# Expert weights in 8 KB pieces, four y buffers, and the residual x in the projections' operand region

## The reference

```python
mod = silu(c) @ ada_w + ada_b                    # shift1, scale1, gate1, shift2, scale2, gate2
u = x * (1 + scale1) + shift1
q, k, v, lru_x, lru_gate, gate_a, gate_b = split(u @ w_in)           # w_in 1024 x 5376
y = sigmoid(gate_a) * sliding_window_attention(q, k, v) \
  + sigmoid(gate_b) * rg_lru(lru_x) * gelu(lru_gate)
x = layer_norm(alpha * x + gate1 * (y @ w_out))
u = x * (1 + scale2) + shift2
# router: softmax(u @ router_w + router_b), one of 4 groups, the 2 best of its 4 experts, weights w
f = sum over the two experts e of w_e * (silu(u @ w_gate[e]) * (u @ w_up[e])) @ w_down[e]
x = layer_norm(alpha * x + gate2 * f)
```

## Time and profile before

| | |
|---|---|
| runs | median 803.24 us (801.51 to 806.11, 3 runs) |
| profiled execution | 802.2 us; from its first to its last instruction 800.0 us |
| mean granted TensorE clock | 0.921 of full |
| busy share | TensorE 82%, VectorE 43%, ScalarE 31%, GpSimd 12% |
| DMA | 189.37 MB, mean 237 GB/s |
| weights' DMAs | 32 each for gate, up and down, 1 MB each; 13.7, 17.3 and 15.1 us from issue to landing (medians) |
| stores of y | 40, 128 KB each |

### The profile page before, as it was taken

The page is one execution under the profiler, slowest core; times in us unless marked ns, Lnnn a source line. Parts: engine busy times, 40 slices in busy tenths (PEclk is TensorE's granted clock), DMA queues, the critical chain, the costliest instruction groups (busy, mean ns, idle before and its releaser), DMA issues.

```text
span 800.0 us, 15178 instructions
## 1 busy us (share of the span) xinstructions
PE 654.3 (82%) x5985; PEld 423.9 (53%) x5986; DVE 341.1 (43%) x657; ACT 251.0 (31%) x522; POOL 97.2 (12%) x184
## 2 busy tenths in 40 slices
PE   0799999999987999999895297979997769999800
PEld 0376666777755777777683144434553334555400
DVE  0355554587888776757545632000110000111148
ACT  0334433747454655545013011111111111111144
POOL 0221000200000000000000231211221111222230
PEclk9999999999989999999996589898998798999955
DMA  9999766461312232237918999999998999982162
GB/s 303 377 282 317 246 237 210 154 215 55 103 54 67 72 90 63 79 106 257 373 53 300 395 346 401 398 353 365 344 341 320 382 329 389 343 307 75 43 215 105
DMA packets 110033, 189.37 MB, mean 237 GB/s; under 512 B 4968, under 2 KB 57416, under 8 KB 106928
## 3 DMA queue, kind: packets, MB, share of 16 engines
q1 hardware_dynamic: 96288, 149.05, 53.4%
q0 software_dynamic: 7264, 31.87, 11.2%
q10 hardware_dynamic: 6448, 8.00, 2.8%
HBM read 175.23 MB, written 13.67 MB: 236 GB/s over the span
## 4 chain that ended last, share of the span: by engine, by line
PE 48%; DMA 18%; DVE 13%; SPq 11%; ACT 5%; issue 4%; POOL 0%; ACTq 0%; POOLq 0%; DVEq 0%
PE psum L1482 11%; DMA wu<-in_moe_w_up_dram 9%; SPq L387 7%; PE psum L1290 6%; DMA raw<-in_w_in_dram 6%; PE psum L1291 6%; PE psum L1292 6%; PE psum L1493 6%; SPq L392 2%; PE psum L1256 2%; SPq L401 1%; PE psum L1333 1%; DMA x<-in_x_dram 1%; PE psum L1465 1%; ACT ssb L729 1%
## 5 line engine op out<-in xcount | busy, mean ns | idle before, releaser
L1482 PE MATMUL psum<-wg,xs 128*32 128x256 f32 x1280 | 158.9, 402 | 27.2 <-DMA wu<-in_moe_w_up_dram 25.3
L1482 PE MATMUL psum<-wu,xs 128*32 128x256 f32 x1280 | 158.3, 402 | 0.0
L1290 PE MATMUL psum<-uh,whi 128*128 128x512 f32 x336 | 137.8, 410 | 1.6 <-DVE wlo L875 1.5
L1291 PE MATMUL psum<-ul,whi 128*128 128x512 f32 x336 | 131.2, 391 | 0.0
L1292 PE MATMUL psum<-uh,wlo 128*128 128x512 f32 x336 | 131.1, 390 | 0.0
L1482 PEld LDWEIGHTS psum<-wg,xs 128*32 128x32 f32 x1280 | 75.1, 114 | 86.3 <-DMA wu<-in_moe_w_up_dram 28.9
L1189 DVE TENSOR_TENSOR h_sb<-psum,hsil 64x256 f32<-64x256 f32 x40 | 17.1, 427 | 187.0 <-ACT hsil L786 187.0
L875 DVE TENSOR_TENSOR wlo<-raw,whi 128x1024 fp32r<-128x1024 f32 x42 | 51.4, 1224 | 69.1 <-ACT whi L613 68.9
L1493 PE MATMUL psum<-wd,hT 128*32 128x256 f32 x1280 | 78.6, 387 | 0.4 <-DVE hT L1193 0.4
L1290 PEld LDWEIGHTS psum<-uh,whi 128*128 128x128 f32 x336 | 63.4, 189 | 22.8 <-issue 7.4
L786 ACT ACTIVATE hsil<-psum 64x256 f32<-64x256 f32 x40 | 15.1, 376 | 187.0 <-PE psum L1482 187.0
(11 more groups left out here) (258 smaller groups left out, 833.1 us busy)
## 6 DMA issues: line engine op xcount, KB each, us to landing
wg<-in_moe_w_gate_dram SPq DMA_DIRECT2D x32, 1024.0 KB, 13.7
wu<-in_moe_w_up_dram SPq DMA_DIRECT2D x32, 1024.0 KB, 17.3
wd<-in_moe_w_down_dram SPq DMA_DIRECT2D x32, 1024.0 KB, 15.1
raw<-in_w_in_dram SPq DMA_DIRECT2D x42, 512.0 KB, 3.9
ada<-in_ada_w_dram POOLq DMA_DIRECT2D x16, 1024.0 KB, 6.8
ada<-in_ada_w_dram SPq DMA_DIRECT2D x8, 1024.0 KB, 17.4
y_d<-ysb ACTq DMA_DIRECT2D x40, 128.0 KB
y_d<-zrow POOLq DMA_DIRECT2D x8, 512.0 KB, 6.4
```

What stands on the lines that cost most here:

```text
L1290: mmul(bank[s % 2], h[:, k, :], uh[:, k, :], start=(k == 0), stop=False)
L1291: mmul(bank[s % 2], h[:, k, :], ul[:, k, :], start=False, stop=False)
L1482: ins = mmul(psum[32 * g:32 * g + 32, 0, 0:256], xs[:, k % 2, k // 2, :], wgu[slot][g // 2][:, k, (g % 2) * 256:(g % 2) * 256 + 256], star ...
```

## The change

1. The contraction orders are turned: partition p holds rows 8p to 8p + 7 of w_gate and w_up (of w_down, two neighbouring rows of each half), so that the part of a 1 MB DMA that goes to one partition is one piece of 8 KB. For this u2 is written in a turned column order, the router's weights are read in the same order, and h is transposed with a step of two.
2. Four y buffers with four semaphores in place of two, and ScalarE's loop goes over four blocks at a time, after four written out ahead of it. The spare rows of y_d are three blocks more, with one more store of zeros.
3. x1 moves from R_Q to R_U (uh's place), and its loads go out as soon as the projections are done, ahead of the weights; slot 0's gate weights move to R_Q, and their first load comes behind the wait for y_lo. Other homes of slot weights and of the last stage's tiles follow.

```diff
@@ homes
-        x1, _ = at(R_Q, "x1", [P, NT, D])
+        x1, _ = at(R_U, "x1", [P, NT, D])
-        for i, o_ in enumerate((R_U, R_Z, R_B)):
+        for i, homes in enumerate(((R_Q, R_U + 16 * KB, R_Y), (R_Z, R_Z + 16 * KB, R_T), (R_B, R_W, R_W + 16 * KB))):
...
-        for i in range(2):
-            t_, o = at(o, f"ysb{i}", [P, 256])
-            ysb.append(t_)
+        ysb = [at(R_W + 32 * KB + KB * i, f"ysb{i}", [P, 256])[0] for i in range(4)]
@@ weights
-        wg_v = moe_w_gate[0].rearrange("e (k p) f -> e p k f", p=P)
-        wu_v = moe_w_up[0].rearrange("e (k p) f -> e p k f", p=P)
-        wd_v = moe_w_down[0].rearrange("e (k p) n -> e p k n", p=P)
+        wg_v = moe_w_gate[0].rearrange("e (p k) f -> e p k f", p=P)
+        wu_v = moe_w_up[0].rearrange("e (p k) f -> e p k f", p=P)
+        wd_v = moe_w_down[0].rearrange("e (a p c) n -> e p a c n", p=P, c=2)
@@ SyncE, behind the projections
             sp.wait_ge(S["proj_ps"], NPROJ)
-            sp.dma_start(a2r[:, :], row_of(3)).then_inc(rows_in, 16)
-            sp.dma_start(b2r[:, :], row_of(1)).then_inc(rows_in, 16)
-            load_gate_up(sp, 0, 0, 0)
-            sp.wait_ge(S["y_lo"], KT)
             for t in range(NT):
                 sp.dma_start(x1[:, t, :], x[0, t * P:(t + 1) * P, :]).then_inc(x1_in, 16)
-
+                if t == 0:
+                    sp.dma_start(a2r[:, :], row_of(3)).then_inc(rows_in, 16)
+                    sp.dma_start(b2r[:, :], row_of(1)).then_inc(rows_in, 16)
+            sp.wait_ge(S["y_lo"], KT)
+            load_gate_up(sp, 0, 0, 0)
             load_gate_up(sp, 0, 0, 1)
@@ ScalarE's loop
-            with act.Fori(2, nblk, 2) as b:
-                gated(b)
-                x_columns(b + 1)
-                y_out(b - 1, 1, b * 8)
-                gated(b + 1)
-                x_columns(b + 2)
-                y_out(b, 0, b * 8 + 16)
+            with act.Fori(4, nblk, 4) as b:
+                for j in range(4):
+                    gated(b + j)
+                    x_columns(b + (j + 1))
+                    if j == 0:
+                        y_out(b - 1, 3, b * 4)
+                    else:
+                        y_out(b + (j - 1), j - 1, b * 4 + 16)
@@ VectorE's u2, TensorE's h_transpose
-                V.scalar_tensor_tensor(u2[t % 2][:, :], zt[:, :], rstd[:, t:t + 1], b2r[:, :], ALU.mult, ALU.add)\
-                    .then_inc(S["u2_done"], 1)
+                V.scalar_tensor_tensor(u2[t % 2][:, :].rearrange("t (k p) -> t p k", k=KT), by_k(zt), rstd[:, t:t + 1],
+                                       by_k(b2r), ALU.mult, ALU.add).then_inc(S["u2_done"], 1)
...
-                    ins = nc.tensor.transpose(bank[2][:, c * 64:(c + 1) * 64], h_sb[64:128, c * P:(c + 1) * P],
+                    ins = nc.tensor.transpose(bank[2][:, c * 64:(c + 1) * 64], h_sb[64:128, bass.ds(c, P, 2)],
                                               ident[64:128, 64:128])
```

More of the change, by code:

```diff
@@ L116, in hybrid_layer @@
     u2_d = dram("u2_d", [T, D])
-    y_d = dram("y_d", [(NBLK + 1) * SUB, D])
+    y_d = dram("y_d", [(NBLK + 4) * SUB, D])
     ctx = ExitStack()
@@ L305, in hybrid_layer @@
         wgu, wdn = [], []
-        for i, o_ in enumerate((R_U, R_Z, R_B)):
-            wgu.append([at(o_ + 16 * KB * m, f"w{'gu'[m]}{i}", [P, KT, FF])[0] for m in range(2)])
-            wdn.append(at(o_ + 32 * KB, f"wd{i}", [P, FT, D])[0])
-        assert R_Z + 48 * KB <= R_T + 16 * KB
+        for i, homes in enumerate(((R_Q, R_U + 16 * KB, R_Y), (R_Z, R_Z + 16 * KB, R_T), (R_B, R_W, R_W + 16 * KB))):
+            wgu.append([at(homes[m], f"w{'gu'[m]}{i}", [P, KT, FF])[0] for m in range(2)])
+            wdn.append(at(homes[2], f"wd{i}", [P, FT, D])[0])
+        assert R_Z + 32 * KB == R_T and R_B + 16 * KB == R_W
         o = R_T + 16 * KB
@@ L319, in hybrid_layer @@
         hT, o = at(o, "hT", [P, 2, 2, SUB])
-        ysb = []
-        for i in range(2):
-            t_, o = at(o, f"ysb{i}", [P, 256])
-            ysb.append(t_)
+        ysb = [at(R_W + 32 * KB + KB * i, f"ysb{i}", [P, 256])[0] for i in range(4)]
         gate2r, o = at(o, "gate2r", [P, D])
@@ L331, in hybrid_layer @@
         fsum = small("fsum", [P, NT, 3])
-        fin = [[at(R_U + 12 * KB * i + 4 * KB * j, f"fin{i}{j}", [P, D])[0] for j in range(3)] for i in range(NT)]
+        fin = [[at(home + 4 * KB * i, f"fin{i}{j}", [P, D])[0] for j, home in enumerate((R_Q, R_U + 16 * KB, R_Y))]
+               for i in range(NT)]
         psum = ctx.enter_context(nc.psum_tensor("psum", [P, 8, 512], F32))
@@ L360, in hybrid_layer @@
         u2_st = [sem(f"u2_st{i}") for i in range(2)]
-        y_st = [sem(f"y_st{i}") for i in range(2)]
+        y_st = [sem(f"y_st{i}") for i in range(4)]
         out_st = sem("out_st")
@@ L390, in load_down @@
             for half in range(2):
-                ks = slice(2 * half, 2 * half + 2)
-                sp.dma_start(wdn[slot][:, ks, :], wd_v[e][:, ks, :]).then_inc(dn_in[slot], 16)
+                sp.dma_start(wdn[slot][:, 2 * half:2 * half + 2, :], wd_v[e][:, half, :, :]).then_inc(dn_in[slot], 16)
         @block.sync
@@ L527, in _ @@
                                            v[0, g * 512:(g + 1) * 512].partition_broadcast(32)).then_inc(late_in, 16)
-                    pool.dma_start(rw[:, :, 0:NE], router_w.rearrange("(k p) e -> p k e", p=P)).then_inc(late_in, 16)
+                    pool.dma_start(rw[:, :, 0:NE], router_w.rearrange("(p k) e -> p k e", p=P)).then_inc(late_in, 16)
                     pool.dma_start(rbr[:, :], router_b.rearrange("(a e) -> a e", a=1)).then_inc(late_in, 16)
@@ L539, in _ @@
                 pool.dma_start(y_d[(NE + 4 * n) * SUB:(NE + 4 * n) * SUB + P, :], zrow[:, :]).then_inc(S["y_zero"], 16)
-            pool.dma_start(y_d[(NBLK - 3) * SUB:(NBLK + 1) * SUB, :], zrow[:, :]).then_inc(S["y_zero"], 16)
-            pool.wait_ge(S["y_zero"], 16 * 8)
+            for b, n in ((NBLK - 3, 4), (NBLK + 1, 3)):
+                pool.dma_start(y_d[b * SUB:(b + n) * SUB, :], zrow[0:n * SUB, :]).then_inc(S["y_zero"], 16)
+            pool.wait_ge(S["y_zero"], 16 * 9)
             for q in u2_st:
@@ L570, in _ @@
             for q in y_st:
-                pool.wait_ge(q, ((nblk + 1) // 2) * 16 + 16)
+                pool.wait_ge(q, ((nblk + 3) // 4) * 16 + 16)
             pool.sem_inc(S["pool_went"], 1)
@@ L617, in split @@
                     act.wait_ge(mod2_out, 16 * 8)
-                    act.wait_ge(S["y_zero"], 16 * 8)
+                    act.wait_ge(S["y_zero"], 16 * 9)
                     if k >= 4:
@@ L791, in x_columns, with y_out @@
                     .then_inc(S["xs_rdy"], 1)
-            def y_out(b, par, stored):
+            def y_out(b, q, stored):
                 act.wait_ge(S["d_ps"], b + 1)
-                act.wait_ge(y_st[par], stored)
-                A(ysb[par][:, :], bank[3][:, 0:256], ACT.Copy).then_inc(S["y_ev"], 1)
+                act.wait_ge(y_st[q], stored)
+                A(ysb[q][:, :], bank[3][:, 0:256], ACT.Copy).then_inc(S["y_ev"], 1)
                 act.wait_ge(S["y_ev"], b + 2)
-                act.dma_start(y_v[:, bass.ds(b * SUB, SUB), :], ysb[par][:, :]).then_inc(y_st[par], 16)
+                act.dma_start(y_v[:, bass.ds(b * SUB, SUB), :], ysb[q][:, :]).then_inc(y_st[q], 16)
             x_columns(0)
[L802 to L806, removed]
+            for b in range(4):
+                gated(b)
+                x_columns(b + 1)
+                if b >= 1:
+                    y_out(b - 1, b - 1, 16)
             act.wait_ge(S["ctrl_done"], 1)
             nblk = act.value_load(ctrl[0:1, NUM:NUM + 1], min_val=NE, max_val=NBLK)
-            with act.Fori(2, nblk, 2) as b:
-                gated(b)
-                x_columns(b + 1)
-                y_out(b - 1, 1, b * 8)
-                gated(b + 1)
-                x_columns(b + 2)
-                y_out(b, 0, b * 8 + 16)
-            pairs = (nblk + 1) // 2
-            y_out(pairs * 2 - 1, 1, pairs * 16)
+            with act.Fori(4, nblk, 4) as b:
[6 more added lines that the diff above has]
+                        y_out(b + (j - 1), j - 1, b * 4 + 16)
+            quads = (nblk + 3) // 4
+            y_out(quads * 4 - 1, 3, quads * 16)
             def weigh(t):
@@ L1042, in _, with by_k @@
                         .then_inc(S["y_lo"], 1)
+            def by_k(row):
+                return row[:, :].rearrange("t (p k) -> t p k", k=KT)
             dve.wait_ge(rows_in, 16 * 3)
@@ L1526, in _ @@
             for done in ("gu_ps", "xT_m_ps", "d_ps"):
-                pe.sem_inc(S[done], 1)
+                pe.sem_inc(S[done], 3)
 _INS = ["x", "c", "ada_w", "ada_b", "w_in", "attn_sink", "rel_bias", "conv_w", "conv_b", "lru_wa", "lru_ba",
```

## The result

The changed kernel takes 809.79 us (median of 7 runs, 806.81 to 812.22) beside 803.24 of the kernel before: ratio 1.008, 95% interval 1.0053 to 1.0107. It is slower, by 6.6 us; the prediction said 811. Its recorded execution took 806.8 us, span 804.7, which is 4.7 us over the span of before; the other 1.9 us of the difference of medians are in no trace.

A forecast was written before the change was run, and what follows sets the result against it. Bound by weights up to expert 12, paced by four engines carrying the y store, then by TensorE. Late y stores outweigh the earlier start and faster pieces: last silu +9.2 us on 802.2 gives 811 us, range 787 to 821.

The forecast's parts named there:

- The two rules: DMA: engine count divides both sides' slowest dimension, so y stores use four engines; each engine takes its queues in turn.
- the sum comes out at 791: Y store on all sixteen engines: 8 pieces each, not 32, giving the stores-keep-pace rival's 791 us; that rival's chance 0.24.
- The start: Before block 0: x's earlier load gains 4.8 us, less 0.7 and 0.4, so block 0 starts 3.7 us earlier.
- turned write of u2: Before gate/up: u2 written at 512 B steps costs 0.7 us each; only tile 3 is on the path.
- The step of two in h: TensorE's 80 loads of h: 1 us taken, bounds zero and 7 us, since waiting blocks hide it.
- The store beside 8 KB pieces: Expert part: a y store takes 32 x (0.312 + 0.046) = 11.5 us, where a block takes 6.1 to 6.5.
- Where ScalarE stands: With four y buffers open, after some nine blocks ScalarE waits in y_out before the copy; idle before silu 9 to 10 us.
- The other sign: Sign of being right: SP's weight issues are short, with 128 pieces each and the ring not full.
- The first run: About blocks 10 to 13: store 4 lands at 529.5, late copies lose 24 us, block 14 ends near 575.
- the 17 us lost up to block 10: Up to block 10: 17 us lost before the change go, weights being ahead of the slowed TensorE.
- The second run: About blocks 24 to 29: 11.5 us a block, weights queued until 697, last silu at 762 instead of 752.79.
- The tail from the last silu to the end: After the last silu: what follows is unchanged.

The follow-up runs named there:

- e1: Changed kernel with each y store issued as four DMAs of 32 partitions, on 16 engines instead of four: 767.3 us, 0.955 of the kernel before.
- e6: Changed kernel with weights in 4 KB pieces instead of 8 KB, and w_down and h as before: 795.4 us, 0.991 of the kernel before.
- e11: Changed kernel with each y store writing half the bytes in as many pieces (512 B for 1 KB): 795.5 us, 0.991 of the kernel before.
- e3: Changed kernel with two y buffers and the two-block loop of before: 821.4 us, 1.023 of the kernel before.
- e12: Changed kernel with eight y buffers, eight semaphores and a loop of eight blocks: 810.6 us, 1.009 of the kernel before.
- e2: Kernel before with only the y store changed, to four DMAs on 16 engines: 780.9 us, 0.972 of the kernel before.

## Why the prediction was right, step by step

**The cause is shown.** It is one store on four engines, turn for turn with pieces of weights. e1 takes the confinement to four engines away (42 us), e6 halves the weights piece (14 us, and the y waits are gone; the step of two went with it), e11 halves the y piece and leaves a store nearly as long. In a slack stretch of the changed kernel, 693 to 697 us, the counts of the two queues are equal, as they were with 2 and 4 KB pieces:

```profile
q1 hardware_dynamic: 48, 0.34, 19.9%
...
q10 hardware_dynamic: 49, 0.05, 3.5%
```

The two rules of the Trainium skill, DMA: Bandwidth & Descriptors, that I set against the change (sections "Why a DMA increments its semaphore by 16 and not by 1" and "Queues, rings and completion order") held: a store whose slowest dimension is 32 on both sides behaves as one on sixteen engines, and engines alternate between queues. The second section gives a packet as some 9 to 17 descriptors; here the turn was one piece of the trace, since from 650.4 to 651.6 us of the kernel before the starts of weights and y pieces alternate one by one without an exception. My sentence that with sixteen engines the sum comes out at 791 was far too high. It took away the waits for y only, not the y pieces' load on the four engines that carry the weights; e1 gives 767.

**The start.** Predicted 3.7 us earlier, measured 3.1 (463.21 against 466.27). x, issued from 369.89 on, landed at 385.06 and not by 380; VectorE finished u2 at 392.73, just as TensorE came to its transposes at 392.79. So the idle time went and the clock stayed up to 400 us, but with no cover left:

```profile
385.06 1.23 DVE L1055 TENSOR_TENSOR row<-psum,row 128x1024 f32<-128x1024 f32 x1 [7.56 <-DMA x<-in_x_dram]
...
390.66 2.07 DVE L1069 SCALAR_TENSOR_TENSOR u<-row,rstd,row 128x1024 f32<-128x1024 f32 x1
```

```profile
380.00:400.00 20.00, 19.89 (x92) 16.28 (x92) 14.42 (x16) 1.56 (x4) 0.00 (x0) 1.00 0.93 386
```

The turned write of u2 takes 2.07 us where before has 1.28 (its four writes: 1283 to 1287 ns): 0.79 more (0.69 in the fourth, which is the one on the path), 0.7 was taken.

**The step of two in h: mis-sized.** I took 1 us out of 0 to 7. A load takes 203 ns for 137, and blocks inside an expert are 6.20 us apart (725.27 to 731.47) where they were 6.09: 39 x 0.11 = 4.3 us if no block hid it.

```profile
L1474 PEld LDWEIGHTS psum<-cst,h_sb x78: 191/203/218, 470.6 to 758.9; 64*128 64x128 f32 x78
```

**The store beside 8 KB pieces: mis-sized the other way.** 11.5 us predicted, 10.7 measured. A turn takes 10.7 / 32 = 0.334 us and not 0.312 + 0.046 = 0.358. Pieces that overlap a little would do that, and DMA's share of 1.02 while it is full points to it, but no run takes the overlap on the four engines alone.

**Where ScalarE stands: half of it was not foreseen.** The prediction has ScalarE wait for a free buffer, 9 to 10 us ahead of each late silu. The runs show two stops of about half that: mostly 3 to 4 us before the copy, for the buffer, and then 5.1 to 6.6 us in the issue of that block's store, so that silu's own idle is 5.7 to 6.9. Two buffers bring the late blocks forward (e3), but eight don't push them back (e12: the first long issue is at 522.39 us, and block 9 is late already, 8.95 us after block 8). So above four the buffers aren't the limit; the issue stops at about the depth that four buffers have. That the two limits lie together, and "four buffers last some nine blocks" came true, is luck. The other sign, short issues of weights by SyncE, came true in part: they took 220 us in all before (455 to 765 us) and 81 now, but 8.84 for two at 535.00.

**The first run came almost to the microsecond.** Store 4 was to land at 529.5 and let block 8's copy go: it went at 530.10. Copies of blocks 9, 10 and 11 were to come at 541, 552 and 564: they came at 541.10, 551.71 and 562.34. There is luck in it: the pieces of the first store, issued at 471.33, started between 475 and 476 us and not at 471, and the shorter stores made up for that. Block 14 was to end near 575; its silu came at 572.96. Of the 17 us lost up to block 10, which were all to go, about 11 went: 463.21 to 536.58 are 73.4 us where ten unhindered steps of 6.2 and six changes make 64. Of the 9.4 that are over, some 4 are new, block 10's late buffer, and the rest is old. The steps to blocks 4 and 5 are still 9.1 and 10.3 us (together 17.8 to 21.0 in every kernel here), with idle of TensorE marked as issue and not as a landing in the changed kernel. What holds them stays open. One candidate that no run varies is the loading of instructions beside a full DMA: their queue moves three pieces of 16 KB between 478 and 500 us, and from there to 765 us none.

**The second run.** Late blocks from 24 to 28 and at 30, as said, but four of them 10.2 to 10.9 us and not 11.5. The last silu came at 756.73, predicted 762: the shorter stores are worth about 0.8 us in each of the late blocks of both runs, nine of them, less the 3.3 us more that the step of two took. That gives 4 of the 5; the rest isn't assigned. The weights were to be queued until 697: DMA was full to 684, and its share was 0.33 from 692 to 700, as if only the lagging engines were still at it.

```profile
676.00:684.00 8.00, 5.03 (x72) 2.55 (x64) 0.43 (x1) 1.14 (x3) 1.49 (x3) 0.93 1.01 423
684.00:692.00 8.00, 8.00 (x106) 4.00 (x108) 0.78 (x3) 1.15 (x3) 1.38 (x3) 0.80 0.70 289
692.00:700.00 8.00, 5.51 (x98) 3.15 (x90) 0.23 (x1) 0.38 (x1) 1.60 (x4) 1.00 0.33 129
```

**The sum.** For the recorded execution the terms gave 811 and it took 806.8, so the model is 4.2 us too slow there. That the median of 809.8 lies nearer is luck. The tail from the last silu to the end was to be unchanged and is 0.8 us longer, unexplained.

**Wrong in the reading of before.** I wrote that TensorE binds from expert 12 on and weights until then, but gave the y store's pieces only 1.5 us of each block's load. That was the right sum and the wrong emphasis: of what was tried here it was the largest thing to be had in the kernel before (22 us, e2), and the change didn't touch it.

## What to carry to other kernels

For a DMA that runs beside a full queue, find out on how many engines it lands and count pieces, not bytes: here a small store on 4 of 16 engines waited one large piece for each of its own, and it slowed the stream on those four, which then set the pace of the whole. Making the stream's pieces larger raised its rate (0.955 with e1 against 0.972 with e2, of which 0.006 is x's) and lengthened the small transfer that shared its engines (from 4.2 us a store, as worked out in the prediction, to 10.7); spread the small one first. More buffers behind a slow store only move the wait, in the end from the landing to the issue.

## What the runs showed of the hardware that was not expected

An issue can hold its engine almost as long as a store takes. With three other stores of 32 pieces an engine open, ScalarE's issue of the next took 5.75 us, and with buffers to spare up to 9.41 (e12); with fewer open mostly 0.55. SyncE shows it too: two w_down issues at 535.00 took 8.84 us in the changed kernel, and before the change, with four times as many pieces in a gate or up DMA, 36 of its 65 rows from 455 to 765 us are over 3 us (6 after it). The nine issues ahead of the silus whose 50.5 us of idle are marked as issue took 47.6 us: these silus waited for their own engine's issue, which the prediction nowhere has.

A step of two float32 numbers is not free on TensorE's weight load (203 against 137 ns for 64 x 128) nor in VectorE's multiply that writes 128 columns apart and reads pairs (642 against 428 ns for 64 x 256). The Trainium skill, SBUF — State Buffer, section Specifications (TRN2), has SBUF read at full bandwidth as long as a 16-byte line is hit at least twice, which a step of two float32 numbers does; here the weight load was half as long again.
